# A hybrid decoder step: loads and softmax of the samples in another order, bias tables in three parts, scores behind a unit's values, a last norm with its sums on ScalarE

## The reference

```
z = x @ w_in                         # one projection, columns shared out to the mixers
A: sparse attention                  # compressed, selected and window branches; 8 heads in 2 groups,
                                     # T5 bias by distance, a gate per branch and head
B: gated DeltaNet;  C: HGRN2
x = LN1(alpha*x + (sum_b sigmoid(gate_b(x)) * (o_b @ w_branch[b])) @ w_out)
x = LN2(alpha*x + MoE(x) + sigmoid(x @ w_ple_gate) * (p @ w_ple))
```

## Time and profile before

| | us |
|---|---|
| median of 3 runs (lowest, highest) | 3167.13 (3161.39, 3167.84) |
| the profiled execution | 3162.14 |
| its span from the first to the last record | 3160.3 |
| opening, from 0 | 142.9 |
| scores of the samples, to 299.0 | 156.1 |
| softmax and values of the samples, to 374.7 | 75.7 |
| prompt, to 705.0 | 330.3 |
| the other stages, to 3070.5 | 2365.5 |
| last norm, to the end | 89.8 |

### The profile page before, as it was taken

The page is one execution under the profiler, slowest core; times in us unless marked ns, Lnnn a source line. Parts: engine busy times, 40 slices in busy tenths (PEclk is TensorE's granted clock), DMA queues, the critical chain, the costliest instruction groups (busy, mean ns, idle before and its releaser), DMA issues. The chain is left out here.

```text
span 3160.3 us, 41309 instructions
## 1 busy us (share of the span) xinstructions
PE 2553.8 (81%) x16047; PEld 2030.9 (64%) x16047; DVE 1327.4 (42%) x2213; ACT 953.4 (30%) x1287; POOL 739.5 (23%) x554
## 2 busy tenths in 40 slices
PE   8897388887975898499456499999898987999960
PEld 8865245557963898499344388888445536787750
DVE  1032256545526665200766211110243107888858
ACT  1100156552231232201442311111000116777740
POOL 2230034433230432422431311110000240101015
PEclk9999579998996899799556699999997998999985
DMA  4454700002101000210001211110212009999973
GB/s 124 109 159 80 139 21 1 1 18 92 46 9 61 1 1 5 87 46 27 3 1 51 97 50 40 40 50 23 93 74 89 0 5 366 401 396 397 390 296 129
DMA packets 82606, 317.45 MB, mean 100 GB/s; under 512 B 14414, under 2 KB 32606, under 8 KB 61782
## 3 DMA queue, kind: packets, MB, share of 16 engines
q1 hardware_dynamic: 56326, 255.72, 22.8%
q10 hardware_dynamic: 17552, 34.47, 3.6%
q0 software_dynamic: 8608, 25.65, 2.3%
HBM read 281.43 MB, written 38.55 MB: 101 GB/s over the span
## 5 line engine op out<-in xcount | busy, mean ns | idle before, releaser
L2377 DVE TENSOR_TENSOR ex_low<-ex_raw,ex_high 128x2048 fp32r<-128x2048 f32 x138 | 308.6, 2284 | 139.6 <-ACT ex_high L2373 138.6
L2373 ACT ACTIVATE ex_high<-ex_raw 128x2048 fp32r<-128x2048 f32 x138 | 256.3, 1910 | 25.8 <-ACT o L2567 15.4
L171 PE MATMUL ps<-mg_high,mg_wg 128*128 128x344 f32 x576 | 191.3, 332 | 41.2 <-POOL mg_wg L1947 41.2
L1007 POOL TENSOR_SCALAR np_z<-np_z,np_sm 128x640 f32<-128x640 f32 (+12 forms) x128 | 128.6, 1022 | 321.2 <-DVE np_sm L978 321.2
L173 PE MATMUL ps<-mg_low,mg_wg 128*128 128x344 f32 x576 | 184.7, 321 | 0.0
L172 PE MATMUL ps<-mg_high,mg_wg 128*128 128x344 f32 x576 | 184.6, 320 | 0.0
L1965 PE MATMUL ps<-o,mg_wb 128*128 128x344 f32 x576 | 170.4, 452 | 0.0
L171 PE MATMUL ps<-hx_high,hgp_w 128*128 128x344 f32 x384 | 123.6, 322 | 42.0 <-DVE hx_low L163 42.0
L2388 PE MATMUL ps<-ex_high,ex_xh 128*128 128x512 f32 x368 | 149.9, 407 | 8.3 <-DVE ex_xl L2611 8.3
L2389 PE MATMUL ps<-ex_high,ex_xl 128*128 128x512 f32 x368 | 146.9, 399 | 0.0
L2390 PE MATMUL ps<-ex_low,ex_xh 128*128 128x512 f32 x368 | 146.6, 398 | 0.0
(11 more groups left out here) (512 smaller groups left out, 6122.9 us busy)
## 6 DMA issues: line engine op xcount, KB each, us to landing
ex_raw<-in_w_eg SPq DMA_DIRECT2D x46, 1024.0 KB, 7.2
ex_raw<-in_w_eu SPq DMA_DIRECT2D x46, 1024.0 KB, 9.4
ex_raw<-in_w_ed SPq DMA_DIRECT2D x46, 1024.0 KB, 9.7
mg_raw<-in_w_mg SPq DMA_DIRECT2D x24, 512.0 KB, 3.6
scratch_s_rows<-o ACTq DMA_DIRECT2D x23, 512.0 KB, 8.7
dnp_w<-in_w_dn SPq DMA_DIRECT2D x16, 512.0 KB, 3.5
hgp_w<-in_w_hg SPq DMA_DIRECT2D x16, 512.0 KB, 3.5
ns_pg<-in_cache ACTq DMA_DIRECT2D x32, 192.0 KB, 2.7
```

The source lines that it names most:

```text
L171: pe.matmul(out, w[:, 0, k, :], x.high[:, k, tokens], start=first, stop=False)
L1007: o = pool.tensor_scalar(zz, zz, sm[:, n % SLOTS, x:x + 1], None, ALU.mult)
L2373: act.activation(self.high[:, q], self.raw[:, q], ACT.Copy).then_inc(self.high_done[q], 1)
L2377: eng.tensor_tensor(self.low[:, q], self.raw[:, q], self.high[:, q], ALU.subtract).then_inc(self.low_done[q], 1)
```

## The change

It has four parts.

1. The eight loads of `vw` go from ACT's queue to SP's, ahead of the table loads.
2. A row of `s_bias` is 2080 elements long instead of 2048, and replica r is stored r + 1 elements to the right, so that the 16 queries of a DMA all read at the same offset, a multiple of 64 B. The table is loaded in three parts of 384 columns, the last columns first and `far` behind the first part, with a semaphore each; the prompt waits for a part when block i = 0, 3, 6 begins.
3. On PE a unit's `turn` and `values` come ahead of the scores that go with it. On DVE the two scalings and the `output` go behind the chunks 0, 1 and 2 of `bias`, one each; `p_sel` is counted per group.
4. In the last norm ACT takes the sum (Copy with accumulation), the mean, the sum of squares (Square with accumulation) and the root; DVE is left with the two additions, the reciprocal and two fused operations (subtract mean and times gain; times reciprocal root and plus shift), two tiles behind the additions; POOL only gathers.

The core of the diff:

```diff
+LBIAS = LSEL + LWIN + 2 * REP
# Opening.scalar
-        act.dma_start(c.dram["s_bias"].rearrange("r h l -> h r l"), self.bv[:].unsqueeze(1).to_broadcast([NH, REP, LSEL + LWIN])).then_inc(s["written"], 16)
+        to = c.dram["s_bias"]
+        act.dma_start(bass.AP(to.tensor, to.offset + 1, [[LBIAS, NH], [NH * LBIAS + 1, REP], [1, LSEL + LWIN]]), self.bv[:].unsqueeze(1).to_broadcast([NH, REP, LSEL + LWIN])).then_inc(s["written"], 16)
# nsa_samples_finish
         @block.sync
         def _(sp):
+            for b in range(NB):
+                sp.dma_start(vw[:, b], dr["state_win"][b].rearrange("(n p) f -> p n f", p=P)[:, :, P:2 * P]).then_inc(s["v"], 16)
             tables.load(sp)
...
         def _(act):
-            for b in range(NB):
-                act.dma_start(vw[:, b], dr["state_win"][b].rearrange("(n p) f -> p n f", p=P)[:, :, P:2 * P]).then_inc(s["v"], 16)
             act.wait_ge(s["zc"], 1)
# Tables
+        def rows_of_queries(dst, at, w, sem):
+            for a in range(P // REP):
+                first = v.offset + at + P - a * REP
+                eng.dma_start(dst[a * REP:(a + 1) * REP], bass.AP(v.tensor, first, [[NH * LBIAS, REP], [LBIAS, NH], [1, w]])).then_inc(sem, 16)
+        for k in range(3):
+            at = self.LM - (k + 1) * self.THIRD
+            rows_of_queries(self.near[:, :, at:at + self.THIRD], at, self.THIRD, self.here[k])
+            if k == 0:
+                rows_of_queries(self.far[:], LSEL, P, self.far_here)
# nsa_prompt, tensor
                 for u in range(max(units, 1)):
-                    for m in before[u]:
-                        scores(n, m)
                     if u < units - 1:
                         turn(f, u)
                     if 0 < u < units:
                         values(f, u - 1)
+                    for m in before[u]:
+                        scores(n, m)
# nsa_prompt, vector (bias calls between[m]() behind chunk m)
             for n in range(N + LAG + 1):
                 if 2 <= n < N + 2:
                     factors(n - 2)
+                later = [lambda g=g: scale(n - 2, g) for g in range(G)] if 2 <= n < N + 2 else []
                 if n > LAG:
-                    output(n - LAG - 1)
+                    later.append(lambda: output(n - LAG - 1))
                 if n < N:
-                    bias(n)
+                    bias(n, later)
...
# last_norm: POOL keeps the gathers alone; DVE runs add(t), finish(t - 2)
+                dve.wait_ge(s["root"], t + 1)
+                dve.reciprocal(stat(t, ROOT), stat(t, ROOT)).then_inc(s["inverse"], 1)
+                link(dve.scalar_tensor_tensor(yy, yy, stat(t, NEG_MEAN), gb[0:r, 0], ALU.add, ALU.mult))
+                dve.scalar_tensor_tensor(yy, yy, stat(t, ROOT), gb[0:r, 1], ALU.mult, ALU.add).then_inc(s["y"], 1)
...
# last_norm, scalar, for each tile, each behind the one before
+                act.activation(junk[0:r], y(t)[0:r], ACT.Copy, accum_out=stat(t, SUM)).then_inc(s["sum"], 1)
+                act.activation(stat(t, NEG_MEAN), stat(t, SUM), ACT.Copy, scale=-1.0 / D).then_inc(s["mean"], 1)
+                act.activation(junk[0:r], y(t)[0:r], ACT.Square, bias=stat(t, NEG_MEAN), accum_out=stat(t, SQUARES)).then_inc(s["squares"], 1)
+                act.activation(stat(t, ROOT), stat(t, SQUARES), ACT.Sqrt, bias=c.eps[0:r], scale=1.0 / D).then_inc(s["root"], 1)
```

More of the change, by code:

```diff
@@ L368, in biases @@
         dr, s = self.c.dram, self.s
-        for t, src in ((self.bs, dr["s_bias"][0, :, P - 1:P + PAST]), (self.bw, dr["s_bias"][0, :, LSEL + P - 1:LSEL + P + WIN])):
+        for t, src in ((self.bs, dr["s_bias"][0, :, P:P + PAST + 1]), (self.bw, dr["s_bias"][0, :, LSEL + P:LSEL + P + WIN + 1])):
             sp.dma_start(t[:], src.unsqueeze(0).to_broadcast([NB, *src.shape])).then_inc(s["bias"], 16)
@@ L777 @@
     LM = PAST + P
-    PIECES = 2 * (P // REP)
+    THIRD = LM // 3
+    BLOCKS = THIRD // P
     def __init__(self, c, sb):
         self.c, self.sb = c, sb
-        self.here = c.sem("np_tables")
+        self.here = [c.sem(f"np_tables{k}") for k in range(3)]
+        self.far_here = c.sem("np_tables_far")
     def allocate(self):
@@ L787, in load, with wait @@
     def load(self, eng):
[L788 to L796, removed]
+        v = self.c.dram["s_bias"]
+        def rows_of_queries(dst, at, w, sem):
[7 more added lines that the diff above has]
+                rows_of_queries(self.far[:], LSEL, P, self.far_here)
+    def wait(self, dve, i):
+        if i % self.BLOCKS == 0:
+            dve.wait_ge(self.here[i // self.BLOCKS], 16 * (P // REP))
+        if i == 0:
+            dve.wait_ge(self.far_here, 16 * (P // REP))
 def spread(parts, among):
@@ L893, in turn @@
                 if m == 0:
-                    pe.wait_ge(s["p_sel"], n + 1)
+                    pe.wait_ge(s["p_sel"], G * (n + 1))
                     pe.wait_ge(s["p"], n + 1)
@@ L936, in _, with bias @@
             dve.tensor_copy(vt[:].rearrange("p k (a b) t -> p (k a) (b t)", a=2), ps[:, 2:6, :]).then_inc(s["vtc"], 1)
-            tables.wait(dve)
-            def bias(n):
+            def bias(n, between):
                 i, j = steps[n]
@@ L942, in bias @@
                 m0 = PAST - i * P
+                if j == 0:
+                    tables.wait(dve, i)
                 mx = sm[:, n % SLOTS, 0:12]
@@ L963, in bias @@
                         o.then_inc(s["drained"], 1)
+                    if m < len(between):
+                        between[m]()
                 dve.wait_ge(s["drained"], G * scored[n + 1])
@@ L978, in factors, with scale @@
                 dve.tensor_tensor(by, by, gates, ALU.mult).then_inc(s["su"], 1)
+            def scale(n, g):
+                a, e = parts(steps[n][0])[SEL]
+                zz, x = z[:, n % SLOTS, g, a:e], 18 + 2 * SEL + g
                 dve.wait_ge(s["su"], n + 1)
[L980 to L984, removed]
+                dve.tensor_scalar(zz, zz, sm[:, n % SLOTS, x:x + 1], None, ALU.mult).then_inc(s["p_sel"], 1)
             def output(n):
@@ L993, in _ @@
                     factors(n - 2)
+                later = [lambda g=g: scale(n - 2, g) for g in range(G)] if 2 <= n < N + 2 else []
                 if n > LAG:
-                    output(n - LAG - 1)
+                    later.append(lambda: output(n - LAG - 1))
+                done = 0
                 if n < N:
-                    bias(n)
+                    bias(n, later)
+                    done = len(chunks(steps[n][0]))
+                for act_on in later[done:]:
+                    act_on()
         @block.gpsimd
@@ L2650, in last_norm @@
     s = Semaphores(c, "ln")
+    RING = 3
+    LAG = 2
     with ExitStack() as ctx:
@@ L2653, in last_norm @@
         gb = sb("gb", [P, 2, D])
-        st = sb("st", [P, 16])
-        er = sb("er", [P, TOPK, 3, D])
+        st = sb("st", [P, NTT, 4])
+        er = sb("er", [P, TOPK, RING, D])
+        junk = sb("junk", [P, D])
         block = ctx.enter_context(nc.Block())
+        SUM, NEG_MEAN, SQUARES, ROOT = range(4)
+        stat = lambda t, k: st[0:rows(t), t, k:k + 1]
         @block.gpsimd
         def _(pool):
[L2660 to L2666, removed]
             for t in range(NTT):
                 r = rows(t)
-                if t >= 3:
-                    pool.wait_ge(s["added"], t - 2)
+                if t >= RING:
+                    pool.wait_ge(s["added"], t - RING + 1)
                 for k in range(TOPK):
[L2673 to L2678, removed]
+                    pool.indirect_dma_start(er[0:r, k, t % RING, :], None, dr["s_rows"], bass.IndirectOffsetOnAxis(rt.dest[0:r, k, t:t + 1], 0))\
+                        .then_inc(s[f"rows{t % RING}"], 16)
         @block.sync
@@ L2704, in _ @@
             for t in range(NTT):
-                root(act, c.eps, st, rows(t), s["asked"], s["given"], t)
+                r = rows(t)
+                act.wait_ge(s["added"], t + 1)
+                if t:
+                    act.wait_ge(s["squares"], t)
+                act.activation(junk[0:r], y(t)[0:r], ACT.Copy, accum_out=stat(t, SUM)).then_inc(s["sum"], 1)
+                act.wait_ge(s["sum"], t + 1)
+                act.activation(stat(t, NEG_MEAN), stat(t, SUM), ACT.Copy, scale=-1.0 / D).then_inc(s["mean"], 1)
+                act.wait_ge(s["mean"], t + 1)
+                act.activation(junk[0:r], y(t)[0:r], ACT.Square, bias=stat(t, NEG_MEAN), accum_out=stat(t, SQUARES)).then_inc(s["squares"], 1)
+                act.wait_ge(s["squares"], t + 1)
+                act.activation(stat(t, ROOT), stat(t, SQUARES), ACT.Sqrt, bias=c.eps[0:r], scale=1.0 / D).then_inc(s["root"], 1)
 def attention(c):
@@ L2866 @@
         "o_dn_p": (P, H4 * P), "o_dn_s": (P, H4 * NB, P), "o_hg_p": (P, H4, P), "o_hg_s": (P, H4 * NB, P)}
[L2867 removed]
+SCRATCH = {"s_gate": ((24, NB), F32), "s_bias": ((REP, NH, LBIAS), F32), "s_x1": ((T, D), F32),
            "s_row": (((EB + 2) * P, 1), U32), "s_rows": ((EB * P, D), F32)}
```

22 lines of the change are left out of this document (15 added, 7 removed).

## The result

The changed kernel takes 3036.4 us, the median of four runs (3027.9 to 3043.7), beside 3165.1 for the kernel before: a ratio of 0.9593, 95% interval 0.9563 to 0.9623. The profiled execution took 3032.8 us with a span of 3030.8, 129.5 less than before. The forecast was 3055 with a range from 3038: the sign and the places were right, the gain was 20 us larger than the sum.

What follows compares the result with a forecast made beforehand. It took ACT's load issuing and the loads' landing to hold the samples' softmax, PE to lead the prompt, DVE to pace the last norm. 47.9 + 32 + 29.7 = 109.6 us off 3162.1 gives 3052.5; stated 3055, range 3038 to 3084.

Steps and rivals of the forecast that it cites:

- the sum of the prompt: Prompt: of 49.9 us of PE's waits for DVE, 32 us would go; bounds 16 and 42.
- the 4.0 and the 2.4: Prompt: new PE waits for ACT's copies, about 0.5 us in 8 steps of blocks 2 and 3, 0.15 in the last 16.
- The walk: Prompt: new order followed through one step, 8.3 us instead of 10.14; ACT's third copy at 6.7, PE wants it at 6.6.
- perhaps 5: Prompt: the granted clock would perhaps rise earlier, worth 5 us; counted only in the range.
- 7.8 + 3.7 = 11.5: Prompt: waits that stay, 7.8 us in steps without a unit to turn, 3.7 in the four one-unit steps.
- 5.48: Last norm: DVE's us per tile after the change, against 8.73 before; the norm ends 29.7 us earlier.
- the forecast's bounds: Whole kernel: time within 3040 to 3066 us by the forecast's own bounds, chance 0.58.
- The finish stage: Softmax and values of the samples: PE's products begin 47.9 us earlier with window loads on SP's queue; bounds 39 and 49.
- both rivals of the write: Opening: slowed bias-row write costs 44 us, 3099, chance 0.06; or makes the kernel slower than before, 3167 or more, chance 0.02.
- Square has no table load of its own: Last norm: rival that Square switches ACT's tables, 5 us less gain, 3060; chance 0.06.
- the bound of the prompt: Prompt: rival that ACT becomes the bound, so the prompt gains 16 us, 3071; chance 0.13.
- The rival of slow loads: Samples' softmax: tables keep 0.119 MB per us and SP's issuing ends the stage, 3061, or window loads are slow, 3064; chance 0.15.

Runs made afterwards that it cites:

- the pieces of 256 columns: Changed kernel plus unread 256-column products in PE's holes (softmax, early prompt), second and third table parts issued in the prompt's block: 3025.7 us, ratio 0.9564.
- part 1 alone: Kernel before with only the window loads moved from ACT's to SP's queue, tables in old layout with one wait: 3145.3 us, ratio 0.9926.
- either side alone: Changed kernel with DVE's order of before in the prompt: 3057.5 us; changed kernel with PE's order of before there: 3058.9 us.

## Why the prediction was wrong

**The step that failed** is the sum of the prompt, "49.9 - 7.8 - 3.7 - 4.0 - 2.4 = 32 us". The mechanism (the scalings and the output between scores and drain) was right. Two terms were not: the 4.0 and the 2.4, new waits of PE for ACT's copies that did not come, and the clock, which the sum puts at nothing. The prompt gained 45.9.

- *The waits for ACT's copies.* The walk gave ACT "two exponentials of 0.91 each". In the kernel before, one begins 0.81 us behind the other in block 4 (512.36 and 513.17); in the changed kernel it is 0.81 there too, 0.71 in block 3 and 0.60 in block 2, where they are 512 and 384 columns wide instead of 640. Block 3 of the changed kernel:

```profile
406.56 0.71 ACT L1039 ACTIVATE np_z<-np_z,np_sm 128x512 f32<-128x512 f32 x1
...
407.27 0.71 ACT L1039 ACTIVATE np_z<-np_z,np_sm 128x512 f32<-128x512 f32 x1
...
408.64 1.13 PE L903 MATMUL ps<-at_z 64*128 64x512 f32 x4
408.68 0.80 ACT L1050 ACTIVATE np_ptb<-ps 128x768 f32<-128x768 f32 x1
409.37 0.36 ACT L1052 ACTIVATE np_ptb<-ps 23x256 f32<-23x256 f32 x1
...
409.78 0.88 PE L928 MATMUL ps<-np_ptb,np_vt 128*64 128x128 f32 x12
```

The second copy ends at 409.73, and PE, busy with scores until 409.77, takes it at 409.78 without a wait. Three exponentials of 0.91 would put the copy 0.6 later, which is the walk's "about 0.5". In block 4 four exponentials at 0.81 bring the third copy from the walk's 6.7 to 6.3, ahead of PE at 6.6. In place of 6.4 us of new waits the old ones fell by 3.7: 10.1 us more than the sum.

- *The clock.* The sum priced the prompt by PE's waits alone and left the clock to the range as "perhaps 5". It was worth 6.9. With the pieces of 256 columns the prompt's own records take 258.4 - 10.4 (the 32 records of filling) = 248.0 us at 1.00. So the low clock cost 272.8 - 248.0 = 24.8 us before and still costs 18.0 after. The products between PE's holes are part of what the holes cost.
- *The waits for DVE that stay.* Here the sum was too kind, by 2.0: 7.8 + 3.7 = 11.5 were forecast and 13.5 came, 5.8 ahead of the first unit, 3.6 in the one-unit steps, 0.75 in blocks 2 and 3 and 3.3 in the last 16 steps, where the walk had none. In block 4 it is the 0.46 us ahead of the fourth chunk, which makes its step 8.77 instead of 8.3.

That is 32 + 10.1 + 6.9 - 2.0 = 47.0, of which 45.9 arrive; the other 1.1 are not traced.

**What else was off.** The last norm gained 3.2 more: a tile is 5.09 and not 5.48, since the four large operations alone fill it (1.28 + 1.28 + 1.26 + 1.28 = 5.10); the reciprocal and the links overlap their neighbours. The untouched stages were 2.9 shorter in this one execution, within their spread of 11. So 3052.5 - 13.9 - 3.2 - 2.9 + 0.1 = 3032.6, against 3032.8 in the profile. On the low side the range took 42 us for the prompt, which are PE's waits for DVE alone; the old waits for ACT, of which 3.7 went, are not in it. And its end does not follow from its own figures: 3040 for the forecast's bounds less 5 for the clock is 3035, and 3038 was stated.

**What was right.** The finish stage: 47.4 of 47.9 in the first profile and 44.5 in the second, by the stated mechanism (the window loads, first in the queue, landed 11.8 us behind their first issue; tables in time; SP's issuing an us ahead). The write of the bias rows: the third weight tile is split at 46.18 (before 46.03), so both rivals of the write fall. Square has no table load of its own, as Copy had none in the earlier trace rows, though the Trainium skill's "Table sets" ("ScalarE: Activation LUTs") does not list it among the fillers. ACT is not the bound of the prompt (186.8 of 286.6 us). The rival of slow loads was right about the rate of the old tables (0.116 MB per us with part 1 alone) and wrong about its price once the tables come in three parts.

**What stays open**: whether the holes of 0.8 to 4.3 us in PE's products with the page values are late loads of instructions; why the tables' rate differs by a factor of up to 1.7 between kernels that load the same rows (1.63 and 0.97 MB in 8 us); whether their layout changes it at all.

## What to carry to other kernels

When holes on PE go, price two things: the holes, and the products between them at the granted clock that they will have then; both can be read from rows at either level. Where two engines pass a pair of buffers back and forth, put independent work of each behind its own half of the exchange: here either side alone gave 30 us and both gave 46. And when a large load is moved ahead of another in one queue, ask what its follower then delays: part 1 alone gained 23 us, and 47 came only with the follower in parts, so that the first user waits only for its own.

## What the runs showed of the hardware

- PE, 81% busy in the prompt's first 50 us (40.1 of 49.6), had a mean granted clock of 0.54 there; with its holes filled by pieces of 256 columns the same steps ran at 1.00.
- The same table rows of 1536 B moved at 0.121 MB per us in one kernel and at 0.204 in another (0.97 and 1.63 MB in 8 us); tables with rows of 4608 B at 0.113 and 0.123 (1.36 and 1.47 MB in 12 us).
- Exponentials with accumulation follow each other on ACT by 0.81, 0.71 and 0.60 us at 640, 512 and 384 columns, less than the 0.82 + 0.19 of the two records that each leaves at 640.
- POOL's indirect DMA issues, 0.94 us each before, took up to 1.80 in the changed norm (mean 1.15), where DVE runs more operations with two tensor sources; that this is the cause was not tested. They were hidden.
